# Attention stages with three score buffers: score matmuls ahead of the transposes on TensorE, and where VectorE copies

## The reference

```python
s_nb = jnp.einsum('brqhd,brkwhd->bhrqkw', qg, k_blk).astype(jnp.float32) * scale
s_nb = s_nb + bias.astype(jnp.float32)[None]
s_nb = jnp.where(in_win[:, None, :], s_nb, -jnp.inf)
s_cx = jnp.einsum('brqhd,bchd->bhrqc', qg, k_ctx).astype(jnp.float32) * scale
...
sc = jnp.concatenate([s_nb.reshape(b, h, rows, GRID_W, n_nb), s_cx], axis=-1)
p = jax.nn.softmax(sc, axis=-1).astype(v.dtype)
```

## Time and profile before

| | |
|---|---|
| median of 3 runs | 4858.2 us (4856.95 to 4863.97) |
| profiled execution, its own time | 4862.26 us |
| its span | 4860.6 us |
| PE busy | 3743.6 us (77%) |
| DVE busy | 2448.4 us (50%) |
| ACT busy | 2216.2 us (46%) |
| mean granted clock of PE | 0.889 |

### The profile page before, as it was taken

One profiled execution on the slowest core, in us unless ns is written; L12 is line 12 of the kernel. 1 busy time (PEld: TensorE's weight loads), 2 busy tenths in 40 slices (PEclk: granted clock), 3 DMA queues, 4 the chain that ended last, 5 costly groups with the idle time before them and its releaser, 6 DMA issues. The chain is left out here.

```text
span 4860.6 us, 70948 instructions
## 1 busy us (share of the span) xinstructions
PE 3743.6 (77%) x24823; PEld 3029.3 (62%) x24823; DVE 2448.4 (50%) x4502; ACT 2216.2 (46%) x3911; POOL 913.2 (19%) x749
## 2 busy tenths in 40 slices
PE   3986786877459999278988869675778997879557
PEld 3974565656348888266766657554656775658446
DVE  2114453442477888475425545455575425546454
ACT  1215454651047777322226657554432226657442
POOL 0213000000026665043540000000034440000002
PEclk7998898988679999689999989887889998989878
DMA  6227413303879999322323242422232223232423
GB/s 218 100 108 224 97 37 77 106 31 131 274 270 391 398 393 345 115 88 83 103 80 70 77 87 57 87 84 76 80 101 67 98 93 76 78 77 58 104 81 94
DMA packets 328087, 634.15 MB, mean 130 GB/s; under 512 B 115048, under 2 KB 171272, under 8 KB 326696
## 3 DMA queue, kind: packets, MB, share of 16 engines
q1 hardware_dynamic: 292436, 510.46, 33.4%
q0 software_dynamic: 33840, 113.66, 7.3%
q10 hardware_dynamic: 1444, 5.30, 0.3%
HBM read 490.39 MB, written 138.95 MB: 129 GB/s over the span
## 5 line engine op out<-in xcount | busy, mean ns | idle before, releaser
L1882 PE MATMUL pr_ps<-pr_wH,hT_part 128*128 128x512 f32 x1120 | 445.6, 398 | 0.0
L1652 ACT ACTIVATE ex_high<-ex_ring 128x2048 fp32r<-128x2048 f32 x192 | 368.6, 1920 | 98.0 <-PE ex_pg L1628 39.6
L1698 DVE TENSOR_TENSOR ex_ring_part<-ex_ring,ex_high 128x2048 fp32r<-128x2048 f32 x144 | 372.4, 2586 | 51.3 <-ACTq L1653 39.6
L1882 PE MATMUL pr_ps<-pr_wH,x_sb_part 128*128 128x512 f32 x896 | 363.9, 406 | 22.5 <-DVEq L1955 22.5
L1882 PE MATMUL pr_ps<-pr_w_part,x_sb_part 128*128 128x512 f32 x896 | 356.6, 398 | 0.0
L1144 DVE TENSOR_REDUCE aa_nm<-aa_ps 128x1 f32<-128x1280 f32 (+1 forms) x144 | 197.7, 1373 | 305.7 <-PE aa_ps L1045 304.9
L1593 POOL TENSOR_TENSOR ex_ring_part<-ex_ring,ex_high 128x2048 fp32r<-128x2048 f32 x48 | 239.3, 4985 | 216.5 <-ACTq L1653 216.5
L1055 PE MATMUL aa_ps<-ident,aa_prob 128*128 128x128 f32 x1312 | 209.0, 292 | 61.8 <-ACTq L1181 60.1
L1177 ACT ACTIVATE aa_prob<-aa_ps,aa_nm 128x512 f32<-128x512 f32 (+2 forms) x272 | 211.1, 776 | 87.9 <-DVEq L1145 44.4
L1144 DVE TENSOR_REDUCE ab_nm<-ab_ps 128x1 f32<-128x1280 f32 (+1 forms) x108 | 148.3, 1373 | 194.7 <-PE ab_ps L1045 194.4
L1882 PEld LDWEIGHTS pr_ps<-pr_wH,hT_part 128*128 128x128 f32 x1120 | 216.5, 193 | 47.1
(11 more groups left out here) (356 smaller groups left out, 9203.6 us busy)
## 6 DMA issues: line engine op xcount, KB each, us to landing
ex_ring<-in_w_gate SPq DMA_DIRECT2D x64, 1024.0 KB, 9.6
ex_ring<-in_w_up SPq DMA_DIRECT2D x64, 1024.0 KB, 8.2
ex_ring<-in_w_down SPq DMA_DIRECT2D x64, 1024.0 KB, 7.9
z_d<-pr_zT POOLq DMA_DIRECT2D x120, 256.0 KB, 3.0
rt_mw<-in_w_ada SPq DMA_DIRECT2D x14, 2048.0 KB, 16.0
pr_w<-in_w_in SPq DMA_DIRECT2D x14, 2048.0 KB, 9.0
mod_w<-in_w_ada SPq DMA_DIRECT2D x10, 2048.0 KB, 13.2
proj<-pr_raw POOLq DMA_DIRECT2D x60, 256.0 KB, 2.3
```

Source lines behind the costliest of these rows:

```text
L1652: scalar.activation(wH[:, c % HL].bitcast(F32R), w_sb[:, c % SL], ACT.Copy)
L1698: vector.tensor_tensor(w_part[:, c % SL].bitcast(F32R), w_sb[:, c % SL], wH[:, c % HL], ALU.subtract)
L1882: mm = tensor.matmul(ps[:, g % 4, :], x.bitcast(F32R), w[:, c % 2, kk, :].bitcast(F32R), start=kk == 0 and i == 0, stop=kk == KC - 1 and i ...
```

## The change

On PE the score matmuls of step h are issued ahead of the transposes of step h - LAG in every stage; before, that was the order with two buffers only. On DVE the copy of step h - LAG comes after the maximum of step h in every stage but ac; before, it came ahead of it in all stages with three buffers. So am and ad change on both engines, ac on PE alone, and aa and ab not at all.

```diff
                     for h in range(n + 4 + LAG):
                         g = h - LAG
-                        if h < n and LAG == 1:
+                        if h < n:
                             scores(h)
                         if 0 <= g < n:
                             transposes(g)
-                        if h < n and LAG == 2:
-                            scores(h)
                         if g % 2 == 0 and g >= 4:
                             turned((g - 4) // 2)
...
                     for h in range(n + 4 + LAG):
                         g = h - LAG
-                        if LAG == 2:
+                        if apart:
                             turned_part(g)
...
                             dve.drain().then_inc(mx, 1)
-                        if LAG == 1:
+                        if not apart:
                             turned_part(g)
```

## The result

The changed kernel took 4915.3 us (median of 4 runs, 4909.6 to 4916.9) against 4860.2 us (4857.0 to 4864.0) for the kernel before in the same measurement: ratio 1.0111, 95% interval 1.0094 to 1.0129. It is 1.1% slower, 55 us. The forecast was 31 us slower.

What follows compares the result with a forecast made beforehand. Loops of waits between engines, followed over one pair of steps, bound the attention stages. am -11, ad -3 and ac +45 us sum to +31: 4889 us for the median, range 4866 to 4925.

Steps and rivals of the forecast that it cites:

- ac's loop: In ac the odd step's scores now stand between values and transposes; pair at full clock from 6.85 to about 7.6 us.
- the side of the result: Whole kernel: slower by more than 0.2% (10 us), chance 0.78.
- One sign: In ac, PE's wait at `turned` grows from 2.57 to about 3.3 us a pair.
- ac's size: ac's two layers lose 45 us: 39 for 42 bound pairs, 3 for other pairs, 3 for the clock; bounds 32 and 78.
- so a few more pairs will see the lower level: 3 us more: In ac, longer PE idle time puts a few more pairs at the lower clock, costing 3 us.
- The second rival: In ac most pairs run values, scores and transposes at 1.2 GHz; ac loses about 78 us, total 4922; chance 0.20.
- the upper bound: ac's loss if every pair goes at the lower clock: 78 us.
- The total: Whole kernel 31 us slower: 4889 us for the median, range 4866 to 4925.
- the first case: Whole kernel: ac loses more than am and ad win, 4868 to 4910 us; chance 0.58.
- am: Stage am: a step loop of PE and DVE remains, pair from 7.98 to 7.58 us, 11 us gained; bounds nothing and 23.
- ad: Stage ad: pair from 7.09 to 7.00 us, odd step 3.32, even 3.68; 3 us gained, bounds nothing and 16.
- The third and fourth rival: Third: am, ad fall to busiest engines' work, 4854 us, chance 0.12; fourth: DVE idle absorbs ac's later transposes, 4844, chance 0.10.

Runs made afterwards that it cites:

- experiments 7 and 8: Extra transposes in ac, and ac's scores without their second product: 7 on the changed kernel, 4848.8 us; 8 on the kernel before, 4850.7 us.
- experiments 5 and 6: 14 extra identity transposes in ac's PE idle time, two waits swapped: 5 on the changed kernel, 4871.4 us; 6 on the kernel before, 4851.4 us.
- Experiment 3: Kernel before, with DVE's maximum ahead of the copy in am and ad, PE as before: 4854.6 us, ratio 0.9991.
- experiment 2: Changed kernel with DVE's copy first again in am and ad, PE's scores still first: 4995.9 us in one run.
- experiment 4: Changed kernel, with the bias and maximum ahead of the copy on DVE in ac too: 4808.4 us, ratio 0.9900.

## Why the prediction was right, and which term was off

- **ac's loop, and the side of the result:** right. The scores stand in the loop (experiments 7 and 8), the transposes start 0.70 us later after `turned` (1.76 for 1.06; forecast 0.75), the pair at full clock takes 7.56 us (forecast 7.6), and PE's wait at `turned` stayed the stage's closing wait: 28 waits and 60.1 us in the first layer, for 29 and 50.5. One sign did not come: at full clock this wait is 2.59 us, not 3.3; 0.50 us of the added idle time stands ahead of the even step's scores.
- **ac's size:** 66 us measured, 45 forecast. "Their cost is 0.75 us at full clock [...] 39 us. The others and the context pairs [...] perhaps 3": at full clock this is 42 x 0.75 + 3 = 35 us, and the order alone costs 29 (experiments 5 and 6), an inner pair 0.63 us. The rest of the 39, 8 us, and "so a few more pairs will see the lower level: 3 us more" make 11 us for the clock, and it cost 37. This is the term that was mis-sized: the forecast charged the lower clock on the scores alone and let its share of the time stay near 30%. In the runs that share went to 46%, and in a pair at the lower clock values, scores and transposes, which are all in the loop, are all slower: 9.4 us for 7.5. Why the share grew as far as it did is not shown. The second rival had this mechanism with its price of 78 us for all pairs; the truth lies between, at 66. On this the Trainium skill ("TensorE: Matmul & The Clock Gate", "Part 1: The HAM clock gate (the "warmup" mystery)", as in the prediction) says that the halved clock is the default and that activity releases it. The runs agree: experiment 5 added only matmuls whose results nobody reads, apart from two waits that changed places, and the granted clock rose from 0.77 to 0.99; and the loss was indeed nearer to the upper bound.
- **The total:** inside the range, with some luck. 4915 lies above the 4868 to 4910 of the first case and 7 us under the 4922 of the second. The clock was 26 us too low; the order in ac, 6 us too high, and the gains of am and ad, 5 us too small (19 us for 14), took 11 off that. 6 us of the 55 lie outside the attention stages and 2 in aa and ab.
- **am:** 8 us gained, 11 forecast. The loop was named rightly; the handover from DVE's copy to PE's scores takes 0.18 us (565.36 to 565.54), not 0.07, the other parts came out within 0.03, and the pair takes 7.72 us, not 7.58. The mistake was to take the distance from ACT's oT to its own copy for a handover from DVE to PE.
- **ad:** 10.5 us gained, 3 forecast. The even step is 3.67 us, as worked out (3.68); the odd one 3.20 instead of 3.32, since scores hand over to transposes after 1.04 us, not 1.10, and the transposes take 1.07 to ACT's copy, not 1.13. That makes 6 us of the 10; the rest lies in the drained ends, where the pair that took 5.3 and 5.6 us now takes 4.0. This rest can't be credited to the change for certain: where ad is the same as before, in experiments 6 and 8, one of these two pairs takes 4.0 us too and ad 246.6, not 250.0.
- **Credit to the wrong edit:** the prediction gave am's gain to both edits together. Experiment 3 shows that DVE's edit alone shortens am's pair, and experiment 2 that PE's edit alone makes am far slower.
- **The third and fourth rival:** am and ad did not fall to their busiest engine's work, and ac did not absorb the transposes' delay. DVE's idle time before its copy in ac was the inside of the loop.
- **Left open:** how far the clock alone explains am in experiment 2, and what sets the share of time at the lower level.

## What to carry to other kernels

Close the loop of waits for one full period and ask of each operation whether it is inside; moving an operation on an in-order engine is free only if it stays outside. When two engines' orders are edited together, time each alone and in the combination that was left out: here the engine that had been left in its old order in one stage turned a gain of 1.0% into a loss of 1.1%. And price PE's idle time twice if PE's own work is in the loop: here the lower clock lengthened just that work and cost more (37 us) than the order (29). A few matmuls without purpose in the idle time, as an experiment, separate the two prices.

## What the runs showed of the hardware

I had not expected how much the lower clock takes with waits at `turned` of mostly 1.9 to 3.3 us in an inner pair: 47 us of the 432 of ac with the new order, given back by 14 transposes a pair (1.69 us). In am with PE's edit alone, with waits at `turned` of mostly 2.1 to 2.2 us, the granted clock was 0.85. From the end of DVE's copy to the first PE matmul that waits for it 0.18 us pass in am and ac alike (565.36 to 565.54 in am of the changed kernel, 3204.00 to 3204.18 in ac of experiment 4).
